# Sine tables of a state-space mixer: the last level shared by two engines, work on them begun earlier, and the output stored in parts

## The reference, cut to what matters

```python
proj = _rmsnorm(h, norm_mix_g[l]) @ w_in[l]          # 1024 -> 512 q, 512 k, 512 v, 512 u
...
# state-space mixer: a linear recurrence with complex decay a = ar + i ai per group and state
step = jnp.exp(log_step)[:, None]
mag = jnp.exp(lr * step)
ar = mag * jnp.cos(li * step)
ai = mag * jnp.sin(li * step)
...
_, _, xr, xi = lax.associative_scan(_complex_affine_combine, (a_r, a_i, bu_r, bu_i), axis=1)
```

## Time and profile before

| | us |
|---|---|
| median of three runs | 5092.28 (5091.86 to 5093.48) |
| the profiled execution | 5092.45 |
| its span in the profile | 5090.7 |
| PE busy | 4680.0 (92%) |
| DVE busy | 2274.5 (45%) |
| ACT busy | 1431.5 (28%) |
| POOL busy | 1936.5 (38%) |

### The profile page before, as it was taken

The page is one execution under the profiler, slowest core; times in us unless marked ns, Lnnn a source line. Parts: engine busy times, 40 slices in busy tenths (PEclk is TensorE's granted clock), DMA queues, the critical chain, the costliest instruction groups (busy, mean ns, idle before and its releaser), DMA issues. The chain is left out here.

```text
span 5090.7 us, 51495 instructions
## 1 busy us (share of the span) xinstructions
PE 4680.0 (92%) x19788; PEld 3545.9 (70%) x19788; DVE 2274.5 (45%) x4548; ACT 1431.5 (28%) x2131; POOL 1936.5 (38%) x884
## 2 busy tenths in 40 slices
PE   7567879999999999999999988899999997787999
PEld 5224757888888888888788745668878873365787
DVE  7787445993333233333440253453233136654440
ACT  2202322334444211111321234332232232233321
POOL 3044413446666444444444400334444431022443
PEclk9788989999999999999999989999999999998999
DMA  3001312445555655555222200212222221011222
GB/s 117 21 25 37 108 37 96 134 137 168 172 178 178 193 190 186 190 188 181 91 96 95 94 23 15 83 65 93 95 91 95 95 83 37 17 58 50 91 94 80
DMA packets 212164, 519.23 MB, mean 102 GB/s; under 512 B 16848, under 2 KB 82640, under 8 KB 208976
## 3 DMA queue, kind: packets, MB, share of 16 engines
q1 hardware_dynamic: 127440, 448.82, 26.9%
q10 hardware_dynamic: 84480, 67.12, 4.2%
HBM read 446.66 MB, written 69.21 MB: 101 GB/s over the span
## 5 line engine op out<-in xcount | busy, mean ns | idle before, releaser
L187 POOL TENSOR_TENSOR ring_rounded<-ring,highs_rounded 128x1024 fp32r<-128x1024 f32 x687 | 1682.1, 2450 | 2756.0 <-ACT highs_rounded L181 2756.0
L370 PE MATMUL bank<-arena_rounded,ring_rounded 128*128 128x512 f32 (+1 forms) x4488 | 1783.8, 397 | 97.3 <-DVE hT_rounded L388 41.4
L372 PE MATMUL bank<-arena_rounded,highs_rounded 128*128 128x512 f32 (+1 forms) x4488 | 1781.9, 397 | 0.0
L181 ACT ACTIVATE highs_rounded<-ring 128x1024 fp32r<-128x1024 f32 x687 | 727.8, 1061 | 2104.6 <-PE bank L372 1610.1
L371 PE MATMUL bank<-hT_rounded,highs_rounded 128*128 128x512 f32 x3128 | 1228.3, 393 | 0.0
L370 PEld LDWEIGHTS bank<-arena_rounded,ring_rounded 128*128 128x128 f32 x4488 | 854.1, 190 | 292.5 <-issue 86.2
L372 PEld LDWEIGHTS bank<-arena_rounded,highs_rounded 128*128 128x128 f32 x4488 | 852.5, 190 | 199.2
L371 PE MATMUL bank<-arena_rounded,highs_rounded 128*128 128x512 f32 (+1 forms) x2112 | 823.9, 390 | 0.0
L371 PEld LDWEIGHTS bank<-hT_rounded,highs_rounded 128*128 128x128 f32 x3128 | 593.3, 190 | 141.5
L371 PEld LDWEIGHTS bank<-arena_rounded,highs_rounded 128*128 128x128 f32 x2112 | 402.2, 190 | 91.0
L1207 DVE TENSOR_TENSOR arena<-qT,arena 128x512 f32<-128x512 f32 x64 | 150.6, 2354 | 372.2 <-ACT qT L1172 371.6
(11 more groups left out here) (319 smaller groups left out, 4727.7 us busy)
## 6 DMA issues: line engine op xcount, KB each, us to landing
ring<-pages_in SPq DMA_DIRECT2D x687, 512.0 KB, 3.4
act_table<-arena SPq DMA_DIRECT2D x128, 256.0 KB, 3.9
gate_table<-qT SPq DMA_DIRECT2D x16, 2048.0 KB, 7.3
arena<-act_table ACTq DMA_DIRECT2D x128, 256.0 KB, 3.9
arena<-gate_table ACTq DMA_DIRECT2D x32, 1024.0 KB, 8.6
arena<-ssm_in SPq DMA_DIRECT2D x16, 256.0 KB, 2.6
arena<-mem_in SPq DMA_DIRECT2D x3, 1024.0 KB, 4.8
xT<-x_in SPq DMA_DIRECT2D x8, 256.0 KB, 6.4
```

The source lines that it names most:

```text
L181: nc.scalar.activation(f32r(page_high(p)), slot(p), ACT.Copy).then_inc(masked_pages.sem, 1)
L187: nc.gpsimd.tensor_tensor(f32r(slot(p)), slot(p), part_of(page_high(p)), ALU.subtract).then_inc(split_pages.sem, 1)
L370: low_last = nc.tensor.matmul(out, f32r(w_low), f32r(x_high), start=start, stop=False)
L372: return low_last, nc.tensor.matmul(out, f32r(w_high), f32r(x_high), start=False, stop=stop)
```

## The change

Four things. The last level of the tables is taken out of `turn_tables` (it now stops at m = 256): for each group of four tables ScalarE makes eight products with the sine of the angle (`upper_products`, 256 columns each, into eight buffers `turned_part`), and VectorE makes the upper halves from them in eight scalar-tensor-tensor instructions (`upper_halves`). The four groups stand ahead of the evictions of the last four blocks. `turn_tables` is begun right behind the sum of squares of the first projection, with 12.0 worth of steps ahead of the root and 4.0 behind it, and is drawn from block 1 on, with a budget of 5.2. In the query projections of the two cross attentions `early` is 1 instead of 2. The last SwiGLU stores each eighth of xT when its addition is done, and the block with the single store is gone. In the projection before the second mixer (`mix_norm0`) the wait for the lambda vectors moves into `gap_of_two`, which by the new rule is drawn from block 1 on.

```diff
+        turned_part = [arena[:, 16640 + 256 * i:16896 + 256 * i] for i in range(8)]
+
+        def upper_products(act, g):
+            act.wait_ge(shifted.sem, shifted.at(g + 1))
+            for t in range(4 * g, 4 * g + 4):
+                nc.scalar.activation(turned_part[2 * (t % 4)], sn(t)[:, 0:256], ACT.Identity, scale=sm[:, t:t + 1])
+                last = nc.scalar.activation(turned_part[2 * (t % 4) + 1], cs[:, t, 0:256], ACT.Identity,
+                                            scale=sm[:, t:t + 1])
+            last.then_inc(exped.sem, 1)
+
+        def upper_halves(dve, g):
+            dve.wait_ge(exped.sem, exped.at(g + 1))
+            for t in range(4 * g, 4 * g + 4):
+                nc.vector.scalar_tensor_tensor(out=cs[:, t, 256:512], in0=cs[:, t, 0:256], scalar=cm[:, t:t + 1],
+                                               in1=turned_part[2 * (t % 4)], op0=ALU.mult, op1=ALU.subtract)
+                last = nc.vector.scalar_tensor_tensor(out=sn(t)[:, 256:512], in0=sn(t)[:, 0:256],
+                                                      scalar=cm[:, t:t + 1], in1=turned_part[2 * (t % 4) + 1],
+                                                      op0=ALU.mult, op1=ALU.add)
+            last.then_inc(shifted.sem, 1)
...
-            while m < SEQ:
+            while m < SEQ // 2:
...
                 m *= 2
+            link.eng.sem_inc(shifted.sem, 1)
...
-                    fetch=None, at_start=False, beside=None, budget=4.6, also=None):
+                    fetch=None, at_start=False, beside=None, budget=5.2, also=None, upper=None):
...
                             high_part(act, done)
                             done += 1
+                        if upper is not None and use >= uses - 4:
+                            upper[0](act, use - uses + 4)
...
                         for j, (x, gain, width, k0, k1, rms) in enumerate(norms):
+                            if j == 0 and at_start:
+                                some(12.0)
                             dve.wait_ge(rooted.sem, rooted.at(ns))
                             token_roots(link, tok(j), bank[7][:, 4 * j:4 * j + tb_all],
                                         width).then_inc(inverted.sem, 1)
+                            if at_start:
+                                some(4.0)
...
-                    if also is not None:
-                        dve.wait_ge(loaded.sem, loaded.at(16))
...
-                                if use >= 4 and (part[0] == "features" or b == 0):
+                                if upper is not None and use >= uses - 4:
+                                    if use == uses - 4:
+                                        some(1000.0)
+                                    upper[1](dve, use - uses + 4)
+                                elif beside is not None and use >= 1 and (part[0] == "features" or b == 0):
                                     some(budget if part[0] == "features" else 3.5 * budget)
...
                     stream(sp, first, pages)
+                    if store:
+                        for d in range(DC):
+                            sp.wait_ge(drawn.sem, drawn.at(d + 1))
+                            sp.dma_start(out[:, d, :], xT[:, d, :]).then_inc(stored.sem, 16)
+                        sp.wait_ge(stored.sem, stored.at(16 * DC))
...
-                        nc.vector.scalar_tensor_tensor(out=xT[:, d, :], in0=bank[(d + 6) % 8][:], scalar=0.5,
-                                                       in1=xT[:, d, :], op0=ALU.mult, op1=ALU.add)
+                        last = nc.vector.scalar_tensor_tensor(out=xT[:, d, :], in0=bank[(d + 6) % 8][:], scalar=0.5,
+                                                              in1=xT[:, d, :], op0=ALU.mult, op1=ALU.add)
+                        if store:
+                            last.then_inc(drawn.sem, 1)
...
-                norms=normed(X, "norm_mix_g", DM, DC), squares=room(14592), at_start=True, beside=turn_tables)
+                norms=normed(X, "norm_mix_g", DM, DC), squares=room(14592), at_start=True, beside=turn_tables,
+                upper=(upper_products, upper_halves))
...
-                    squares=room(0))
+                    squares=room(0), early=1)
...
             for j in range(2):
+                if j == 0:
+                    link.eng.wait_ge(loaded.sem, loaded.at(16))
...
-        swiglu(1, 1)
+        swiglu(1, 1, store=True)
...
-        with nc.Block() as block:
-            @block.sync
-            def _(sp):
-                sp.dma_start(out, xT[:]).then_inc(stored.sem, 16)
-                sp.wait_ge(stored.sem, stored.at(16))
```

More of the change, by code:

```diff
@@ L441, in project @@
             tb_all = n // P
+            uses = sum(p[1] * (ns if p[0] == "features" else 1) for p in parts)
             def tok(j):
@@ L592, in _, with some @@
                     link = Dve(dve, dve_step)
+                    steps = beside(link) if beside is not None else iter(())
+                    def some(us):
+                        while us > 0:
+                            used = next(steps, None)
+                            if used is None:
+                                break
+                            us -= used
                     if norms is not None:
@@ L660, in project @@
                 exped.close(1)
-            uses = sum(p[1] * (ns if p[0] == "features" else 1) for p in parts)
+            if upper is not None:
+                exped.close(4)
+                shifted.close(5)
             full.close(uses)
@@ L1076, in stick_breaking, with swiglu @@
             made.close(1)
-        def swiglu(layer, half_):
+        def swiglu(layer, half_, store=False):
             norm_of = f"ffn_norm{layer}{half_}"
```

10 lines of the change are left out of this document (2 added, 8 removed).

## The result

The changed kernel takes 5055.34 us (median of four executions, 5048.88 to 5057.54) against 5092.07 before (5090.55 to 5093.48): ratio 0.9926, 95% interval 0.9909 to 0.9943. The forecast was 5067.5 us, 5058 to 5079. The profiled execution took 5057.54 us with a span of 5055.7, 35.0 us less than the 5090.7 of before; the forecast had 24.8. The other 2 us of the 12 are that the profiled execution is the slowest of the four.

What follows compares the result with a forecast made beforehand. VectorE, making the sine and cosine table at the end of the first projection, was taken as the bound. From 5092.45 us, 19.0 (first stage), 3.0 (means) and 2.8 (store) gave 5067.7, or 5067.5 against the median; range 5058 to 5079.

Steps and rivals of the forecast that it cites:

- And about 4 either way for stretches of low clock that shift.: Whole program: shifting low-clock stretches widen the range by about 4 us either way, with no term in the sum.
- The store, -2.8: Program end: eight 256 KB stores follow the additions, the last landing 3.9 us after issue; -2.8 us, bounds 1.5 and 3.8.
- The first stage, -19.0.: First projection: table work begun earlier and last level shared; stage end at 146.5 against 165.5, -19.0 us.
- The sharing itself thus gains nothing here.: Last table level: shared by ScalarE and VectorE it takes 32.0 us, against 31.0 before.
- Without these two collisions it would gain 4.: Last table level: without GpSimd's two operations (2 x 2.4 us) in VectorE's first two groups, sharing would gain 4 us.
- The means, -0.7 and -2.3.: Cross query projections of layers 0 and 1: mean products one block earlier gain 0.7 and 2.3 us; bounds 0 and -5 together.
- The range.: Whole time: 5058 to 5079 us around 5067.5, for the case as summed, chance 0.84.
- At no cost: Projection with lambda (mix_norm0): small work moves from block 5 to block 1 without costing time.
- (b): First stage: TensorE's new wait leaves its clock low and TensorE bounds; 5094 us, no measurable change; chance 0.08.
- (c): Output: the eight stores land one after the other, 3.9 us each, +19 instead of -2.8; 5089 us; chance 0.05.
- (d): TensorE-bound first stage, then low clock through head norm and first attention heads: slower, 5114 us; chance 0.03.

Runs made afterwards that it cites:

- the one small square: Kernel before plus one unused 16-column ScalarE square ahead of layer 1's first feed-forward block; 5084.46 us against 5092.51, ratio 0.9985.
- the store kernel: Kernel before with only the output stored in eight parts; median 5086.98 us, ratio 1.0003.

## Why the prediction was wrong, point by point

- **"And about 4 either way for stretches of low clock that shift."** This step failed, and it is the largest part of the miss: 6.9 us at projections that the change does not touch, where the sum has nothing. I took shifting low stretches for a symmetric noise around 0. The runs show an effect of the change: with layer 0's early products the gain drops by 0.4 us across the low stretches of that layer (20.39 to 19.98; without them it doesn't), and the last of these ends 0.2 us earlier in the work (at 3343.07 instead of 3343.25, in the time of before's trace). So the work behind comes later against it by about as much as the one small square's 0.24, and the fall of the clock 850 us on is gone in all eight traces. Before itself has two outcomes there, 0 and 3.4 (traces without the early products: three each), so the gain there is 3.5 or 6.9, and the first trace of before is of the kind that makes it 6.9. The whole miss between the profiled executions, 10.2 us, is this 6.9, 1.8 of the store, 1.1 of the first stage (where the clock of the first 30 us gave 1.8), 1.2 of layer 1 and -0.9 of layer 0.
- **The store, -2.8 with 1.5 and 3.8 as bounds.** A term mis-sized beyond its bounds: 4.6. I took 3.9 us to landing from stores that share their queue with a stream of pages; at the end of the program no page moves (0 GB/s from 5040 to 5047), and 256 KB land in 2.1. That the traffic makes the difference is argued from this, not tested. The figure of the Trainium skill ("DMA: Bandwidth & Descriptors", section on one DMA's anatomy: 2.0 us and bytes over 436 GB/s, stated for transfers that GpSimd issues, while SyncE issues these) gives an estimated 2.6 us, 4.4 for 1 MiB and 6.8 for 2 MiB, where the rows show 2.1, 3.9 and, before, 6.3: the slope agrees, the fixed part is 1.5 here. It was the better guide of the two.
- **The first stage, -19.0.** Right, and right in its steps: the last level at 114.30 for 114.5, alternating groups, two of VectorE's instructions lengthened by 2.1 us, TensorE waiting and catching up. Span to span it is 20.1, like with like 18.1 to 18.3. That the number 19.0 lies between them is in part luck: the execution profiled before had the low clock in its first 30 us, that of the changed kernel had not.
- **"The sharing itself thus gains nothing here."** Wrong, though the sum was not. I compared the shared level with the 31.0 us of before. Begun earlier, an unshared level takes 38.1 us, because TensorE's starved blocks and their evictions fall into it. With sharing they lie under the alternation. Like with like the earlier start alone gains 8.8, the shared level alone some 6, both together 18.3: sharing adds 9.5 to the earlier start.
- **"Without these two collisions it would gain 4."** Right: the alternation without them measured 29.0 with two page copies of 0.96 on ScalarE's path, so an estimated 27.0 without, 4.0 below the 31.0 of before.
- **The means, -0.7 and -2.3.** Layer 0's sign was wrong: TensorE's new wait is 2.58 us (2.7 forecast), but it leaves the clock low (the row below, of the changed kernel), the bound that I had named (0). Layer 1: 2.0 at the evictions (2.3 forecast), and 1.5 more in the head norm behind.

- **The range.** Its terms, added straight, reach from 5050.5 to 5084.7; 5058 to 5079 took for granted that they do not all fall to one side. The terms for the store and for the low stretches each went past their own bound, both to the fast side.
- **"At no cost"**, of the wait for the lambda vectors, held: the difference of the two traces stays constant to 0.3 us over that stage.
- **The rivals** (b), (c) and (d) did not come. For (b) the wait did lower the clock (0.59 from 64 to 80), but it is 0.93 from 80 to 109; for (c) the stores land at 2.1 us each, overlapping.

```profile
3244.00:3252.00 8.00, 8.00 (x34) 6.52 (x34) 0.83 (x5) 1.21 (x2) 2.37 (x1) 0.79 0.04 4
```

## What to carry to other kernels

Cost a moved piece of work against what the schedule would be without its companion change, not against the old schedule: the sum had sharing at -1.0 us against the old schedule, and it was worth 9.5 on top of the earlier start. Take a transfer's time from a row with the same traffic around it. Two engines that hand buffers to each other and use all of them at once pay the sum of both; two halves of the same buffers made it nearly the longer one, for 7.6 us here.

## What the runs showed that I had not expected

In this program the places where the granted clock falls are tied to the work: in the traces with the late products it falls in layer 0's head norm and attention at the same instructions to 0.3 us, whatever the executions differ in before, and in those with the early products at a second fixed set. Most of the difference between executions arises in the first 680 us (1.8 to 2.0 us by the clock at 20 to 28, and from 3.6 us lost to 9 gained against the first trace between 166 and 680, in the head norm and attention of the first mixer); the rest is two steps of 1.5 us at 2457 and 2830 and the 3.4 at the latent-attention projections. A delay of 0.24 us moved 7 us of gain into a place 400 us later, and one of 1.3 us in the changed kernel took 4 away. What remains open is why before itself gives 0 in some executions and 3.4 in others, and what the three executions of the store kernel above 5105 us were; no trace of one was taken. So a difference of 7 us in this kernel, though reproducible, says nothing of whether an edit is good: it must be read from the place that the edit touches.
